# The 512-token norms are handed to the next stage in two halves of 256 tokens, four weight tiles take each half, and GpSimd makes half of the low parts

## What is computed

```python
def rms_norm(x):
    xf = x.astype(jnp.float32)
    return (xf * lax.rsqrt(jnp.mean(xf * xf, axis=-1, keepdims=True) + EPS)).astype(x.dtype)

def modulate(h, shift, scale):
    return h * (1 + scale[:, None, :]) + shift[:, None, :]

for layer in range(DEPTH):                       # DEPTH = 2
    mx = jnp.split(jax.nn.silu(c) @ ada_w[layer] + ada_b[layer], N_MOD, axis=-1)   # mc: the same of c_ctx
    x = x + 0.5 * mx[2] * swiglu(modulate(rms_norm(x), mx[0], mx[1]), ffn1_w_gu, ffn1_w_down)   # and ctx
    hx = modulate(rms_norm(x), mx[3], mx[4]); hc = modulate(rms_norm(ctx), mc[3], mc[4])
    x = x + mx[5] * merge_mixers(attention, pool, fourier of hx @ w_in)            # and ctx unless last
    x = x + 0.5 * mx[8] * swiglu(modulate(rms_norm(x), mx[6], mx[7]), ffn2_w_gu, ffn2_w_down)   # and ctx unless last
```

## Time and profile before

| | before |
|---|---|
| time of three runs (us) | 3000.35, 3000.7, 2998.56; median 3000.35 |
| the profiled execution: its time, its span (us) | 3005.61, 3003.9 |
| mean granted TensorE clock (share of 2.4 GHz) | 0.98 |
| TensorE busy | 2853.6 us, 95% |
| VectorE, ScalarE, GpSimd busy | 50%, 39%, 7% |

### The profile page before, as it was taken

One profiled execution on the slowest core, in us unless ns is written; L12 is line 12 of the kernel. 1 busy time (PEld: TensorE's weight loads), 2 busy tenths in 40 slices (PEclk: granted clock), 3 DMA queues, 4 the chain that ended last, 5 costly groups with the idle time before them and its releaser, 6 DMA issues. The chain is left out here.

```text
span 3003.9 us, 46242 instructions
## 1 busy us (share of the span) xinstructions
PE 2853.6 (95%) x18122; PEld 2485.5 (83%) x18122; DVE 1492.0 (50%) x2045; ACT 1182.7 (39%) x1717; POOL 197.6 (7%) x224
## 2 busy tenths in 40 slices
PE   7999999889999989999989999999999999998998
PEld 4777876567777867788769998899999999998998
DVE  3323233552323252332555558774566577659764
ACT  3222222442322132321344445553645445455553
POOL 0000011100000000000110002200300000003000
PEclk9999999999999999999999999999999999999999
DMA  6545224024544233532315553455445565552553
GB/s 236 182 154 183 97 100 148 28 70 154 182 149 139 96 123 141 187 102 97 107 50 194 186 176 106 135 188 191 147 154 189 167 193 210 190 172 95 168 191 131
DMA packets 120366, 443.63 MB, mean 148 GB/s; under 512 B 13440, under 2 KB 14848, under 8 KB 119616
## 3 DMA queue, kind: packets, MB, share of 16 engines
q1 hardware_dynamic: 119248, 431.38, 42.2%
q0 software_dynamic: 1008, 10.75, 0.9%
HBM read 441.03 MB, written 1.05 MB: 147 GB/s over the span
## 5 line engine op out<-in xcount | busy, mean ns | idle before, releaser
L1562 DVE TENSOR_TENSOR wlo<-raw,whi 128x1024 fp32r<-128x1024 f32 x672 | 828.0, 1236 | 978.1 <-ACT whi L1116 976.6
L1116 ACT ACTIVATE whi<-raw 128x1024 fp32r<-128x1024 f32 x672 | 706.7, 1054 | 1023.7 <-PE ps L494 635.2
L492 PE MATMUL ps<-nh,whi 128*128 128x512 f32 (+1 forms) x1696 | 626.0, 369 | 39.4 <-DVE wlo L1562 19.2
L493 PE MATMUL ps<-nl,whi 128*128 128x512 f32 (+1 forms) x1696 | 614.9, 363 | 0.0
L494 PE MATMUL ps<-nh,wlo 128*128 128x512 f32 (+1 forms) x1696 | 613.9, 362 | 0.0
L492 PE MATMUL ps<-bh,whi 128*128 128x256 f32 x1664 | 483.1, 290 | 9.4 <-DVE bl L1649 7.0
L493 PE MATMUL ps<-bl,whi 128*128 128x256 f32 x1664 | 472.8, 284 | 0.0
L494 PE MATMUL ps<-bh,wlo 128*128 128x256 f32 x1664 | 472.6, 284 | 0.0
L492 PEld LDWEIGHTS ps<-nh,whi 128*128 128x128 f32 x1696 | 324.3, 191 | 147.2 <-DVE wlo L1562 53.8
L494 PEld LDWEIGHTS ps<-nh,wlo 128*128 128x128 f32 x1696 | 324.0, 191 | 49.8
L493 PEld LDWEIGHTS ps<-nl,whi 128*128 128x128 f32 x1696 | 324.6, 191 | 45.7 <-issue 0.2
(11 more groups left out here) (214 smaller groups left out, 3040.1 us busy)
## 6 DMA issues: line engine op xcount, KB each, us to landing
raw<-stream SPq DMA_DIRECT2D x800, 512.0 KB, 3.7
head<-stream SPq DMA_DIRECT2D x8, 1024.0 KB, 15.1
gates_w<-gate_in POOLq DMA_DIRECT2D x2, 3328.0 KB, 13.1
cst<-cst_in POOLq DMA_DIRECT2D x2, 1280.0 KB, 5.9
X<-x_in SPq DMA_DIRECT2D x1, 2048.0 KB, 8.0
out<-X SPq DMA_DIRECT2D x8, 128.0 KB, 2.0
fftw<-fftw_in POOLq DMA_DIRECT2D x2, 256.0 KB, 5.9
ws<-ws_in POOLq DMA_DIRECT2D x1, 512.0 KB, 3.9
```

Source lines behind the costliest of these rows:

```text
L492: pe.matmul(dst, w1, rhs_hi, start=start, stop=False)
L493: pe.matmul(dst, w1, rhs_lo, start=False, stop=False)
L1116: act.activation(whi[:, at % RING, :], raw[:, n % RING, :], ACT.Copy).then_inc(w_hi_ready, 1)
L1562: dve.tensor_tensor(wlo[:, r, :], raw[:, PLACE["main", at] % RING, :], whi[:, r, :].bitcast(F32), ALU.subtract).then_inc(w_ready, 1)
```

## The change

1. The 512-token norms run for all k on the x half (columns 0 to 255), then for all k on the context half. Between the halves ScalarE and VectorE split one more weight slot, so that four are ready.
2. For odd k ScalarE makes, behind `nh`, a second full copy of y + shift in `tmpa` (`full_ready`), and GpSimd subtracts `nh` from it (`odd_lower`, `nl_odd_ready`). Even k stay with VectorE.
3. TensorE takes the x half for four tiles, then the context half (`first_four`, `half_pair`), in `ffn1_up0`, `in0`, `ffn2_up0` and `ffn1_up1`; in `in1` it does so for two tiles.
4. Since four main slots must be in `raw` before the first pass, the ada slots stand later in `ORDER` (`ADA_LOADED`, `IN_ADA_LOADED`), and the first group of each stage issues the pairs 0 and 1 one right behind the other. In `in0` the splits run three slots ahead and not one, pair n follows tile n + 2, and ScalarE copies the conditioning row (`ada_row`) ahead of its split.
5. The late split of a slot stands behind the inversion of the norm's sums on VectorE. Where splits are issued in the "up" stages moves by one place over the loop's edge, in the same order.

```diff
+IN_ADA = {3: (0, 1), 4: (2,), 5: (3,), 6: (4,), 7: (5,), 8: (6,), 9: (7,)}
+ADA_LOADED = {4: 0, 5: 1, 6: 2, 7: 3}
+IN_ADA_LOADED = {4: (0,), 5: (1,), 6: (2,), 7: (3,), 8: (4,), 9: (5, 6, 7)}
...
-                if _m in ADA_AFTER:
-                    _ada([_at + ADA_GROUP.index(("ada", 2 * ADA_AFTER[_m] + _n)) for _n in range(2)])
+                if _m in ADA_LOADED:
+                    _ada([_at + ADA_GROUP.index(("ada", 2 * ADA_LOADED[_m] + _n)) for _n in range(2)])
...
+            def half_pair(at, b, h, joint):
+                weights(at + 1)
+                part = slice(h * S, (h + 1) * S)
+                steps = [(k, n) for k in range(KD) for n in range(2)]
+                if not joint:
+                    steps.sort(key=lambda step: step[1])
+                for k, n in steps:
+                    if joint and n == 0:
+                        if k % 2:
+                            pe.wait_ge(nl_odd_ready, c["odd"] - KD + h * (KD // 2) + k // 2 + 1)
+                        else:
+                            pe.wait_ge(nl_ready, c["nl"] - KD + h * (KD // 2) + k // 2 + 1)
+                    last = mm3(ps[:, b + n, part], at + n, k, nh[:, k, part], nl[:, k, part], k == 0, k == KD - 1)
+                    if h and k == KD - 1:
+                        last.then_inc(slots_done, 1)
+
+            def first_four(at, unit):
+                for h in range(2):
+                    for q in range(2):
+                        if h == 0:
+                            pe.wait_ge(up_evac, unit + q + 1)
+                        half_pair(at + 2 * q, 2 * q, h, q == 0)
...
+                        if first:
+                            first_four(at, unit)
+                            for n in (2, 3):
+                                ada_pair(KD * g, ADA_AFTER[n], i)
...
-                joint_tiles(bank(0), in_slot(l, 0), bank(1), in_slot(l, 1), 0, T)
+                if l == 0:
+                    first_four(in_slot(l, 0), c["unit"] - 1)
+                else:
+                    half_pair(in_slot(l, 0), 0, 0, True)
+                    half_pair(in_slot(l, 0), 0, 1, True)
...
+                for h in range(w // S):                      # ScalarE
+                    part = slice(h * S, (h + 1) * S)
+                    for m in range(KD):
+                        act.wait_ge(y_ready, c["y"] + m + 1)
+                        act.activation(dst[:, m, part], tmpb[:, m % 2, part], ACT.Identity,
+                                       bias=mod[:, ord_shift, m, h:h + 1]).then_inc(nh_ready, 1)
+                        if w == T and m % 2:
+                            c["full"] += 1
+                            if c["full"] > 2:
+                                act.wait_ge(nl_odd_ready, c["full"] - 2)
+                            act.activation(tmpa[:, m // 2 % 2, part], tmpb[:, m % 2, part], ACT.Identity,
+                                           bias=mod[:, ord_shift, m, h:h + 1]).then_inc(full_ready, 1)
+                    c["y"] += KD
+                    if w == T and h == 0:
+                        split_to(c["split"])
...
-                    split_to(in_slot(l, i) + (3 if l else 1))
+                    if l == 0 and i in (6, 9):
+                        ada_rows(c["ada"], 0)
+                        c["ada"] += 1
+                    split_to(in_slot(l, i) + 3)
...
                 add_last(w)                                  # VectorE
+                inv_of_sums(w)
                 late_split()
-                inv_of_sums(w)
...
+            def odd_lower():                                 # GpSimd, behind norm_squares
+                for h in range(2):
+                    part = slice(h * S, (h + 1) * S)
+                    for m in range(1, KD, 2):
+                        c["full"] += 1
+                        pool.wait_ge(full_ready, c["full"])
+                        pool.tensor_tensor(nl[:, m, part], tmpa[:, m // 2 % 2, part], nh[:, m, part].bitcast(F32),
+                                           ALU.subtract).then_inc(nl_odd_ready, 1)
```

More of the change, by code:

```diff
@@ L1228, in ffn_up @@
                 local = 0
+                if w == S:
+                    split(at + 3)
                 if ada_groups:
@@ L1622, in norm_mod @@
                 dve.wait_ge(rows_ready, c["root"])
-                def lower(m):
-                    dve.wait_ge(nh_ready, c["y"] + m + 1)
-                    for s, part in enumerate(halves(w)):
-                        last = dve.scalar_tensor_tensor(
-                            out=nl[:, m, part], in0=tmpb[:, m % 2, part], scalar=mod[:, ord_shift, m, s:s + 1],
-                            in1=nh[:, m, part].bitcast(F32), op0=ALU.add, op1=ALU.subtract)
-                    last.then_inc(nl_ready, 1)
@@ L1632, in norm_mod @@
-                for m in range(KD):
-                    if m >= 2:
-                        dve.wait_ge(nl_ready, c["y"] + m - 1)
-                    for s, part in enumerate(halves(w)):
-                        last = dve.scalar_tensor_tensor(
-                            out=tmpb[:, m % 2, part], in0=X[:, m, part], scalar=fix[:, scale_at, m, s:s + 1],
-                            in1=ps[:, 7, part], op0=ALU.mult, op1=ALU.mult)
-                    last.then_inc(y_ready, 1)
-                    if m:
-                        lower(m - 1)
@@ new lines, in norm_mod @@
+                if w == S:
+                    for m in range(KD):
+                        if m >= 2:
+                            dve.wait_ge(nl_ready, c["nl"] + m - 1)
+                        y(m, 0)
+                        if m:
+                            lower(m - 1, 0)
+                    lower(KD - 1, 0)
+                    c["y"] += KD
+                    c["nl"] += KD
+                    return
+                for h in range(2):
+                    for m in range(KD):
+                        if m >= 2 and m % 2:
+                            dve.wait_ge(full_ready, c["odd"] + m // 2)
+                        elif m >= 2:
+                            dve.wait_ge(nl_ready, c["nl"] + m // 2)
+                        y(m, h)
+                        if m % 2:
+                            lower(m - 1, h)
+                    c["y"] += KD
+                    c["nl"] += KD // 2
+                    c["odd"] += KD // 2
+                    if h == 0:
+                        split_to(c["split"])
@@ L1736, in up4 @@
                          between=lambda: split(at + 4 + 2 * q, dyn))
+                    if not mlp:
+                        split(at + 5 + 2 * q, dyn)
                     if mlp:
```

103 lines of the change are left out of this document (63 added, 40 removed).

## The result

The changed kernel took 3021.16 us (median of 4 runs, 3013.75 to 3023.28) beside 2999.89 for the kernel before: ratio 1.0063, 95% interval 1.0046 to 1.0081. It is slower, by 19 us, and lies above the forecast range of 3000 to 3017. With five more rounds (first experiment) it took 3016.77 for 3003.73, ratio 1.0038, interval 1.0025 to 1.0051. The profiled span grew from 3003.9 to 3021.6. The profiled executions of the changed kernel are the slowest of their samples, 3023.28 in the first and 3023.69 in the second, so its traces stand 2 and 7 above the medians.

The account below looks back on a forecast made before the run. TensorE, busy 95% of the span, was taken as the bound. Four first passes +18.8, `wlo` in three stages -16.4, `in0` +0.6, `in1` +5.8, late split -0.4 gave +8.4: 3009 us for 3000.35, range 3000 to 3017.

Parts of the forecast that it names:

- Start by halves: Five norms: TensorE starts 1.73 us after the first y, for 2.93; a gain of 1.2 each.
- 192 halves: Four-tile first passes: 192 matmuls of 256 columns replace 96 of 512, costing 1.1 us in each of four stages.
- Stops behind pair 0: Four stages: TensorE stands for the load of pair 1's second slot, costing 3.5 us each.
- The clock behind them: Four stages: TensorE runs at half clock after the stop for pair 1, costing 1.3 us each, bounds 0 and 3.2.
- `wlo` waits: Main slots loaded ahead of ada slots remove 16.4 us of waits in three up stages, and 2.9 in `in0`.
- The late split (-0.4): Split moved behind the inversion in each norm: 0.1 us gained in four, -0.4 in all.
- End of `in0`: Rotations start 7.9 us behind the last tile, costing 5.0; GpSimd's pool sums slow four rotations, costing 2.0.
- `in1`, +5.8: `in1`: first pass 1.0 us later, a wait of 3.4 for GpSimd's late loads, and 1.4 of lower clock.
- GpSimd's part: One GpSimd subtraction of 256 columns per two k takes 1.10 us, under the 1.6 available, so it costs nothing.
- rival D: First passes: GpSimd and VectorE hinder each other, low parts come slower than TensorE takes them; 3018 us, chance 0.14.
- Rival B: Stops come without the lower clock, or the tail of `in0` is hidden; 3002 us, chance 0.24.
- C: Rival: pair 1's second slot is there when TensorE wants it, so the stops are short; 2992 us, chance 0.10.

Follow-up runs that it names:

- first experiment: The changed kernel timed again with no edit, five rounds beside the kernel before: 3016.77 us, ratio 1.0038.
- spread and mended: Changed kernel with one pair behind each tile (5 and 6 behind tile 8 in `in0`), capped splits in `in0`, GpSimd's loads before its subtractions: 2983.21 us, ratio 0.9932.
- the order alone: Kernel before with only the load table changed, each pair of ada slots one main slot later in the three up stages: 2985.31 us, ratio 0.9936.
- the loads together: Changed kernel with only the load order changed, pair 1's two ada slots loaded straight behind pair 0's: 3003.93 us, ratio 0.9997 to the kernel before.

## Why the prediction came out as it did

The direction was right, the mechanisms were those forecast, and the size was too small by 9 us against the span and 12 against the first median; the interval of the second measurement takes the forecast in. The step that failed is the price of the lower clock: the sum had 5.5 for it, the trace has 20.9. Step by step:

- **Start by halves, -1.2 each.** 1.78 of standing for 2.97: right. The sum took it that the lower clock ends earlier by as much. In `in0` it ended at 454.54 before and at 454.22 after, so TensorE, starting 1.24 earlier, works 0.9 longer at half clock. This place differs from trace to trace (3.4 to 6.1 at half clock behind the start in the ten traces with halves, 4.2 to 5.3 in the three without). Over the five passes it is 18.8 to 22.9 without halves and 21.0 to 26.3 with them, on average 0.5 longer a pass, so that some 0.3 of each 1.2 is given back; the ranges overlap.
- **192 halves, +1.1 per pass.** 24 of 256 columns start 0.1200 apart, and the four tiles of `in0` end at 473.9, forecast 473.6. Kernels with and without halves (spread and mended against the order alone) differ in the column "all else" by 0.4, 1.1 and 1.2 in the three up stages, but the changed kernel and the kernel before with only its loads reordered by 0.6, 0.3 and -0.1. So a pass costs 0.3 to 0.9 more, at or under the forecast. An estimate by the Trainium skill ("TensorE: Matmul & The Clock Gate", Back-to-back issue gap) is that two halves cost 2.5 ns more than a whole; these rows have 13.5.
- **Stops behind pair 0, +3.5.** 3.37, 3.42, 3.47, 3.46: right.
- **The clock behind them, +1.3.** This is the term that was mis-sized. It came from a single row at half clock, 3.42 long behind a stop of 2.4; a stop of 3.5 brought 6.83, and 2.8 to 3.1 lost. Filling it gave back 10.4, or 2.6 for each, for 5.2 in the sum. The other support, the stop of 2.97 ahead of the pass in `in0`, was no case of a single stop: the clock had fallen at 444.30, behind an earlier wait of 2.5 and before that stop began.
- **`wlo` waits, -16.4.** Gone; the order alone was worth 18.4. In `in0` the waits of 2.9 and 2.4 are gone too, and the half clock from 495.50 with them, 1.7 for the forecast 1.1. The late split (-0.4) can't be seen apart from the rest.
- **End of `in0`.** The rotations start 8.2 behind the last tile (forecast 7.9), and GpSimd's contention is there (2.23 where 0.42 would do). The rotations' products take 7.3, for 4.3 before: 3.0 where the sum had 2. The sum had +7.0 for both; undoing it took 10.1 in the trace, 6.3 of it waits, and 3.2 is again clock, behind waits that I counted as time alone.
- **`in1`, +5.8.** The wait was 2.9 (forecast 3.4) and the loads landed 5.7 to 5.8 after issue (5.9). `in1` grew by 8.2; undoing the late loads took 7.2 in the trace, 4.1 of it clock where the sum had 1.4.
- **GpSimd's part, nothing.** A subtraction lasts 0.74, under the 1.10 of the earlier trace rows. Right, and rival D is out: no wait for a low part in any pass of four tiles.
- **Rival B** had it the other way round. Half clock was not less than I took, but more. **C** is out by the stops.

In all, the clock came out 15.4 over the sum. Of these 6.5 lie behind the four stops, 3.2 at the end of `in0`, 2.2 in `in1` and some 3 at the starts of the passes. The other terms together came out 6.1 lower than forecast (+2.9 forecast, -3.2 measured), and so the miss is 9 and not 15. Of the 6.1, 0.8 is the first start (2.0 earlier for 1.2) and 5.4 lie in the three up stages, where waits and the rest fell by 11.6 for a forecast 6.2. There the reordered loads alone took off 18.8 for 16.4, and what the halves and the stops added was 7.2 for 10.2, mostly since the halves cost less than 1.1 a pass. What is left in the other stages nearly cancels.

Open is why the changed kernel measured 1.0063 once and 1.0038 the other time; the two intervals overlap from 1.0046 to 1.0051. Single executions ran from 3013.75 to 3023.28 and from 3011.92 to 3023.69, and in both samples the fastest execution had a higher mean granted clock than the slowest (0.977 for 0.973, and 0.977 for 0.975), so part of it may be how often the clock fell; that is not shown.

## What to carry to other kernels

Price a new stop of the busiest engine at its length plus what the clock costs behind it; here a stop of 3.5 cost about 6. A wait can move its cost from "waiting" to "busy" in the profile, so compare the busy time of the same work and the granted clock by stage, not the waits alone. And test the cheap part alone: the whole gain that was had here came with one table of load positions (0.64%; 0.70% with one line moved as well, which is no clear difference), and the handover by halves with all its mends gave nothing beyond it (0.68%).

## What was not expected of the hardware

- How the clock answers to a stop is not a matter of its length alone. Behind stops on `raw` of 0.82, 0.93, 0.93, 1.35 and 1.57 no stretch at half clock followed, and none behind one of 2.83 in `in0`; behind one of 2.10 there were 3.41, and behind the eighteen of 3.2 to 3.7 there were thirteen times 6.83, four times 3.41 and once nothing.
- The same instructions can meet a different clock: `in1` had 23.9 us at half clock in the changed kernel and 11.1 in the run with the loads together, whose order of loads differs in the stages ahead of it, 5.9 us of span, with no instruction of its own changed.
- A product of two SBUF operands on VectorE took 2.23 across a GpSimd instruction of the same kind that lasts 2.40, and 0.41 or 0.42 without one, a factor of five. The trace thus agrees with the Trainium skill ("GPSIMD Engine Reference", Specifications), which names contention of GpSimd with VectorE instructions of two SBUF inputs.
